# The four residual norms of a three-layer network kernel: the last tile's sums read from its PSUM bank, the sums of seven tiles placed within the last weight chunk, and the VectorE chain rewritten without operations on two SBUF operands

## The chip, the core and the metric

The kernel runs on one core of one Trainium2 chip. The metric is the device time of one execution in microseconds (us), as the median of repeated runs; lower is better.

## The reference, cut to what matters

The program is a network of three layers on 512 tokens with a model width of 1024, all in fp32. The first two layers end each of their halves in a normed, gated residual; the second half of the chain is the norm ahead of the next projection:

```
def rms_normalize(x):
    xf = x.astype(jnp.float32)
    return xf * lax.rsqrt(jnp.mean(xf * xf, axis=-1, keepdims=True) + EPS)

for i in range(DEPTH):                       # DEPTH = 2
    h = rmsnorm(x, norm_g[i, 0]) * (1.0 + scale) + shift
    y = short_conv_mixer(...) if i == 0 else ssd_mixer(...)
    x = x + gate * rmsnorm(y, norm_g[i, 1])
    h = rmsnorm(x, norm_g[i, 2]) * (1.0 + scale2) + shift2
    y = swiglu_ffn(h, f_w_in[i], f_w_out[i])
    x = x + gate2 * rmsnorm(y, norm_g[i, 3])
```

So there are four places, here called norm 0 to norm 3, at which a projection y (8 tiles of 128 channels by 512 tokens) becomes the new x, and the new x is normalised for the next projection. A third layer (attention and a gated FFN) follows, with norms of another form that the change does not touch.

## The kernel before, in words

Activations lie with the channels on the 128 partitions and the tokens along the free axis; a tile is 128x512. A projection multiplies fp32 weights in three products (high part by high part, high by low, low by high), so one tile with 8 k tiles takes 24 matmuls of 128x512. Weights stream through a ring of 4 chunks: SP loads `raw`, ScalarE writes the rounded part `whi` (`split_hi`), GpSimd writes the rest `wlo` (`split_lo`, 128x1024), and TensorE's `chunk` waits for it. Each engine has its own instruction list in program order, written by hand, and the lists meet only at semaphores.

A projection's tile m goes to bank `(T0 + m) % 4`. At the end of the four projections with a residual norm (`a_out`, `f_out0`, `m_out`, `f_out1`), ScalarE (`y_out`) squares tile m from the bank, writes y = gate column times the bank, and squares y; VectorE (`residual_sums`) forms x*y and adds three running sums over the tiles: `sums[0]` of the raw squares, `sums[1]` of x*y, `sums[2]` of y squared. For tile 7 the squares are added into `sums[0]`, while x*y stays in `ta` and the square of y in `tb`.

Then comes the chain of the norm. TensorE (`residual_roots`) sums over the channels with `token_sums`: the data is the stationary operand and a column of ones moves, 4 matmuls per buffer, each of which the trace shows as two records. There are five such buffers: `sums[1]`, `sums[2]`, `sums[0]`, `ta`, `tb`. ScalarE takes the square root of the first sum; VectorE inverts it (`R1`), squares the inverse (`R1SQ`), and combines the sums into the mean square of the new x (`PART`, `LAST`, `ssum`), without waiting for the new x itself; ScalarE takes that root, and VectorE inverts it (`R2`). TensorE spreads `R1` and `R2` over the partitions (`spread`, 4 matmuls of 128x128 each, in two records apiece) into banks 6 and 4. VectorE then forms, for each k, `grown` (y times bank 6, into `sq`), `added` (x plus that) and `scaled` (x times bank 4), ScalarE writes `h_hi` and `tb` from it, and GpSimd `h_lo`. TensorE takes them in the order of k in `four`, whose first matmul (line 566) waits for the first `h_hi`; it also waits for the low parts of the next projection's first four chunks.

In ScalarE's list `y_tile` sets, for the last tile, `y_out`, then one `split_hi`, and after it the roots:

```
done(c + chunks - 1)
y_out(name, r, m, y, sums)
split_hi(c + RING + chunks - 1)
```

Of the kernel before, what the change touches and what calls it, by code (L numbers as in the profile page):

```python
# [25 lines left out]
P = 128  # L26
# [97 lines left out]
def program(nc, io):  # L124
    with ExitStack() as ctx:
# [26 lines left out]
        root = sb("root", [P, 7, NT])  # L152
# [92 lines left out]
        s_done, s_ready, std_out, r_ready, rb_done = (sem(n) for n in ("s_done", "s_ready", "std_out", "r_ready", "rb_done"))  # L245
# [85 lines left out]
        STD, R1, R1SQ, PART, LAST, R2, SPARE = range(7)  # L331
# [199 lines left out]
        def _(pe):  # L531
            PRODUCTS = ((whi, "hi"), (whi, "lo"), (wlo, "hi"))

            def chunk(c, it, n, bank, ktiles, k0, xs, first, last, wait_in=None):

                s = c % RING
                pe.wait_ge(lo_ready, c + 1 + it * n)
                for kk in range(ktiles):
                    k = k0 + kk
                    if wait_in is not None:  # L540
                        pe.wait_ge(in_ready, wait_in + k + 1)
                    for i, (w, part) in enumerate(PRODUCTS):
                        mm = nc.tensor.matmul(psum[bank][:], w[:, s, kk, :], xs[part == "lo"][:, k, :],  # L543
                                              start=first and kk == 0 and i == 0,
                                              stop=last and kk == ktiles - 1 and i == 2)
                mm.then_inc(chunk_done, 1)
# [8 lines left out]
            def single(name, u, it=0, n=0, xs=(h_hi, h_lo), wait=True, c=None):  # L555

                b = bank_of(T0[name] + u, it, n)
                chunk(C0[name] + (u if c is None else c), it, n, b, CH, 0, xs, True, True, I0[name] if wait else None)
# [36 lines left out]
            def down(name, it, xs):  # L595

                for m in range(4):
                    b = bank_of(T0[name] + m, it, 4)
                    k = 0
                    for u, n in enumerate((6, 5, 6, 5)):  # L600
                        chunk(C0[name] + 4 * m + u, it, 16, b, n, k, xs, u == 0, u == 3, I0[name] if m == 0 else None)
# [17 lines left out]
            def residual_roots(r, sums):  # L619

                pe.wait_ge(acc_c, 6 * (r + 1))
                token_sums(5, sums[:, 1, :], True)
                token_sums(4, sums[:, 2, :], True)
                pe.wait_ge(acc_a, 7 * (r + 1))
                token_sums(6, sums[:, 0, :], True).then_inc(s_done, 1)
                pe.wait_ge(xy_out, r + 1)
                token_sums(5, ta[:, 1, :], False).then_inc(s_done, 1)
                pe.wait_ge(yc_out, KD * (r + 1))
                token_sums(4, tb[:, 1, :], False).then_inc(s_done, 1)
# [58 lines left out]
            for u in range(KD):  # L688
                single("a_out", u, xs=(g_hi, g_lo))
                if u == 0:  # L690
                    modulation(10)
            residual_roots(0, sums)

            def ffn(n):
# [21 lines left out]
                with pe.Fori(0, 2) as it:  # L716
                    down(f"f_out{n}", it, (g_hi, g_lo))
                residual_roots(1 + 2 * n, sums)
# [117 lines left out]
            for m in range(4, KD):  # L836
                b = bank_of(T0["m_out"] + m)
                for u in range(2):
                    chunk(C0["m_out"] + 2 * m + u, 0, 0, b, CH, CH * u, (m_hi, m_lo), u == 0, u == 1)
            residual_roots(2, sums_m)  # L840
# [194 lines left out]
        def _(act):  # L1035
# [25 lines left out]
            def residual_roots(r):  # L1061

                act.wait_ge(s_done, sums_done(r, 0))
                take_root(roots(r, 0), psum[6][:, 0:NT])
# [33 lines left out]
            def y_out(name, r, m, y, sums):  # L1098
# [5 lines left out]
                if m >= 3:  # L1104
                    act.wait_ge(acc_a, 7 * r + m - 2)
                dst = sq[:, m % 2, :] if m else sums[:, 0, :]
                nc.scalar.activation(dst, psum[b][:], ACT.Square).then_inc(ya_out, 1)  # L1107
                nc.scalar.activation(y[:, m, :], psum[b][:], ACT.Identity, bias=zcol[:], scale=ncol[:, r, 1, m:m + 1]).then_inc(bank_free[b], 1)
# [372 lines left out]
        def _(dve):  # L1481
# [21 lines left out]
            def residual_sums(name, r, y, sums):  # L1503

                for m in range(KD):
                    t = T0[name] + m
                    if m:
                        dve.wait_ge(ya_out, KD * r + m + 1)
                        if m >= 2:
                            dve.wait_ge(acc_a, 7 * r + m - 1)  # L1510
                        TT(sums[:, 0, :], sums[:, 0, :], sq[:, m % 2, :], ALU.add).then_inc(acc_a, 1)  # L1511
                    read_out(t)
                    if m == KD - 1:
                        TT(ta[:, 1, :], x[:, m, :], y[:, m, :], ALU.mult).then_inc(xy_out, 1)
                        return
                    step(TT(ta[:, m % 2, :] if m else sums[:, 1, :], x[:, m, :], y[:, m, :], ALU.mult))
                    if m:
# [4 lines left out]
                        TT(sums[:, 2, :], sums[:, 2, :], tb[:, m % 2, :], ALU.add).then_inc(acc_c, 1)  # L1522

# [12 lines left out]
            def residual(r, i, phase, y):  # L1536

                inverse(roots(r, 0), R1)
                step(TT(root[:, R1SQ, :], root[:, R1, :], root[:, R1, :], ALU.mult))
                dve.wait_ge(s_done, sums_done(r, 1))  # L1540
                step(STT(out=root[:, PART, :], in0=psum[5][:, 0:NT], scalar=2.0, in1=root[:, R1, :], op0=ALU.mult, op1=ALU.mult))
                step(TT(root[:, PART, :], root[:, PART, :], ssum[:], ALU.add))
                dve.wait_ge(s_done, sums_done(r, 2))
                step(TT(root[:, LAST, :], psum[4][:, 0:NT], root[:, R1SQ, :], ALU.mult))
                TT(ssum[:], root[:, LAST, :], root[:, PART, :], ALU.add).then_inc(s_ready, 1)
                inverse(roots(r, 1), R2)

                def grown(k):
                    return step.note(TT(sq[:, k % 2, :], y[:, k, :], psum[6][:], ALU.mult))

                def added(k, v):
                    step.wait(v)
                    return step.note(TT(x[:, k, :], x[:, k, :], sq[:, k % 2, :], ALU.add))  # L1553
# [148 lines left out]
            residual(0, 1, "f_in0", y)  # L1702

            def ffn(n):
# [33 lines left out]
                residual(1 + 2 * n, 2 + 2 * n, ("m_in", "w_in")[n], y)  # L1738
# [166 lines left out]
            residual(2, 3, "f_in1", y_m)  # L1905
# [300 lines left out]
```

## Time and profile before

| | |
|---|---|
| time, median of 3 runs | 2298.25 us (2295.49 to 2298.49) |
| time of the profiled execution | 2297.04 us |
| its span, first to last instruction | 2295.2 us |
| mean granted TensorE clock | 0.978 |
| TensorE matmul busy | 2223.1 us (97%), 10434 instructions |
| VectorE busy | 1242.6 us (54%) |
| ScalarE busy | 994.1 us (43%) |
| GpSimd busy | 974.2 us (42%) |

The profiled execution lasted 1.84 us longer than its span. TensorE is nearly always busy. The stretches of the four norms lie at 226 to 238 us, 622 to 635 us, 1100 to 1112 us and 1484 to 1496 us of the span. The granted clock is given as a share of full speed: 1.00 is 2.4 GHz, 0.50 is 1.2 GHz. The program's other time is the same loop of weight chunks and the third layer's attention.

### The profile page before, as it was taken

The numbers are of one execution on the slowest core, as the hardware profiler recorded it, in microseconds if no ns is written. First come the engines' busy times: TensorE is split into PE (matmuls) and PEld (weight loads), VectorE is DVE, ScalarE is ACT, GpSimd is POOL, SyncE is SP. The second block draws the span as 40 slices with busy tenths as digits, with TensorE's granted clock in tenths as the row PEclk, the third lists the DMA queues.
The fourth block names the chain that finished last, engine by engine and source line by source line (L and its number), as shares of the span: only waits on it lengthen the run. The fifth ranks groups of instructions, "written<-read, shape, count | busy, mean of one in ns | idle before, by whom it ended". The sixth has DMA issues, their size and how long they took to land.

```text
span 2295.2 us, 28959 instructions
## 1 busy us (share of the span) xinstructions
PE 2223.1 (97%) x10434; PEld 1761.0 (77%) x10434; DVE 1242.6 (54%) x1718; ACT 994.1 (43%) x1420; POOL 974.2 (42%) x421
## 2 busy tenths in 40 slices
PE   6999999999979999989999999999999899999998
PEld 4788888788867777767788888878677688888886
DVE  5876666521297787786522221250777755666412
ACT  4324443333435546554534334453555634444332
POOL 3544443446534333334444446556211143444563
PEclk8999899999989999999899999999999999999999
DMA  7553475553315344332133223334321032333232
GB/s 304 212 202 125 152 265 201 185 143 95 115 40 186 111 142 149 113 111 90 59 103 97 91 72 95 109 106 145 97 67 47 29 107 76 108 93 91 76 91 72
DMA packets 74096, 273.83 MB, mean 119 GB/s; under 512 B 8519, under 2 KB 11207, under 8 KB 67736
## 3 DMA queue, kind: packets, MB, share of 16 engines
q1 hardware_dynamic: 70632, 266.74, 35.6%
q10 hardware_dynamic: 3376, 5.90, 0.8%
q8 instruction: 57, 0.93, 0.2%
q14 instruction: 31, 0.25, 0.0%
HBM read 269.21 MB, written 8.12 MB: 121 GB/s over the span
## 4 chain that ended last, share of the span: by engine, by line
PE 76%; issue 14%; POOL 5%; DVE 3%; ACT 1%; DMA 0%; ACTq 0%; POOLq 0%; SPq 0%; DVEq 0%
PE bank L543 60%; POOL wlo L504 5%; PE bank L913 4%; PE bank L566 2%; PE bank L1006 2%; PE bank L970 1%; PE bank L934 1%; PE bank L953 1%; PE bank L570 1%; PE bank L607 1%; PE bank L615 1%; PE bank L654 1%; PE bank L854 0%; DVE x L1553 0%; DMA ada_first<-ada_d 0%
## 5 line engine op out<-in xcount | busy, mean ns | idle before, releaser
L504 POOL TENSOR_TENSOR wlo<-raw,whi 128x1024 fp32r<-128x1024 f32 x382 | 928.8, 2438 | 1235.9 <-ACT whi L1044 1235.7
L1044 ACT ACTIVATE whi<-raw 128x1024 fp32r<-128x1024 f32 x382 | 401.3, 1055 | 622.9 <-PE bank L543 588.3
L543 PE MATMUL bank<-h_hi,whi 128*128 128x512 f32 x1616 | 649.3, 402 | 4.9 <-DVE dt_tok L1878 2.5
L543 PE MATMUL bank<-h_hi,wlo 128*128 128x512 f32 x1616 | 638.1, 395 | 0.0
L543 PE MATMUL bank<-h_lo,whi 128*128 128x512 f32 x1616 | 636.0, 394 | 0.0
L543 PEld LDWEIGHTS bank<-h_hi,whi 128*128 128x128 f32 x1616 | 303.9, 188 | 79.6 <-issue 5.7
L543 PEld LDWEIGHTS bank<-h_hi,wlo 128*128 128x128 f32 x1616 | 303.8, 188 | 77.2
L543 PEld LDWEIGHTS bank<-h_lo,whi 128*128 128x128 f32 x1616 | 304.0, 188 | 70.4
L543 PE MATMUL bank<-g_hi,whi 128*128 128x512 f32 x592 | 236.3, 399 | 0.0
L543 PE MATMUL bank<-g_hi,wlo 128*128 128x512 f32 x592 | 233.2, 394 | 0.0
L543 PE MATMUL bank<-g_lo,whi 128*128 128x512 f32 x592 | 232.1, 392 | 0.0
L1713 DVE TENSOR_TENSOR tb<-ta,bank 128x512 f32<-128x512 f32 x44 | 30.1, 685 | 222.3 <-PE bank L543 202.7
L1495 DVE TENSOR_TENSOR g_lo<-tb,g_hi 128x512 f32 (+1 forms) x52 | 109.1, 2098 | 51.9 <-ACT g_hi L1173 45.0
L543 PEld LDWEIGHTS bank<-g_hi,wlo 128*128 128x128 f32 x592 | 111.1, 188 | 29.1
L543 PEld LDWEIGHTS bank<-g_lo,whi 128*128 128x128 f32 x592 | 111.1, 188 | 26.4
L543 PEld LDWEIGHTS bank<-g_hi,whi 128*128 128x128 f32 x592 | 111.1, 188 | 25.4
L1511 DVE TENSOR_TENSOR sums<-sums,sq 128x512 f32<-128x512 f32 x21 | 14.5, 692 | 193.2 <-ACT sq L1107 193.1
L1652 DVE SCALAR_TENSOR_TENSOR tb<-bank,vec,tb 128x511 f32<-128x511 f32 (+1 forms) x140 | 104.8, 749 | 9.8
L566 PE MATMUL bank<-h_hi,whi 128*128 128x512 f32 x160 | 68.2, 426 | 9.2 <-ACT h_hi L1089 7.0
L1843 DVE TENSOR_TENSOR csb<-csb,cbm 128x1280 f32<-128x1280 f32 x32 | 72.0, 2288 | 0.3
L519 POOL TENSOR_TENSOR h_lo<-tb,h_hi 128x512 fp32r<-128x512 f32 x35 | 45.2, 1293 | 59.9 <-ACT tb L1090 59.6
L566 PE MATMUL bank<-h_hi,wlo 128*128 128x512 f32 x160 | 67.2, 420 | 0.0
(337 smaller groups left out, 2953.5 us busy)
## 6 DMA issues: line engine op xcount, KB each, us to landing
raw<-f_in_d SPq DMA_DIRECT2D x88, 512.0 KB, 3.5
raw<-m_d SPq DMA_DIRECT2D x65, 512.0 KB, 3.7
ada_f<-ada_d SPq DMA_DIRECT2D x24, 1024.0 KB, 7.0
raw<-g_in_d SPq DMA_DIRECT2D x44, 512.0 KB, 3.5
raw<-w_in_d SPq DMA_DIRECT2D x41, 512.0 KB, 3.6
csb<-cs_d SPq DMA_DIRECT2D x32, 640.0 KB, 6.5
ada_a<-ada_d SPq DMA_DIRECT2D x16, 1024.0 KB, 4.9
raw<-a_in_d SPq DMA_DIRECT2D x24, 512.0 KB, 6.0
```

The source lines that it names most:

```text
L504: nc.gpsimd.tensor_tensor(wlo[:, s], raw[:, s], whi[:, s].bitcast(F32), ALU.subtract).then_inc(lo_ready, 1)
L519: nc.gpsimd.tensor_tensor(h_lo[:, k, :], tb[:, k % 2, :], h_hi[:, k, :].bitcast(F32), ALU.subtract).then_inc(in_ready, 1)
L543: mm = nc.tensor.matmul(psum[bank][:], w[:, s, kk, :], xs[part == "lo"][:, k, :], start=first and kk == 0 and i == 0, stop=last and kk == ...
L566: nc.tensor.matmul(psum[tiles[i]][:], w[:, (C0[name] + i) % RING, k, :], h_hi[:, k, :], start=k == 0 and j == 0, stop=False)
L570: mm = nc.tensor.matmul(psum[tiles[i]][:], whi[:, (C0[name] + i) % RING, k, :], h_lo[:, k, :], start=False, stop=k == KD - 1)
L913: mm = nc.tensor.matmul(psum[7][:], w[:, c % RING, m // 3, :], (h_hi, h_lo)[part == "lo"][:, m // 3, :], start=m == 0, stop=m == 23)
L1006: mm = nc.tensor.matmul(psum[b][:], w[:, c % RING, k, :], (h_hi, h_lo)[part == "lo"][:, k, :], start=kk == 0 and i == 0, stop=kk == 3 and ...
L1044: nc.scalar.activation(whi[:, s], raw[:, s], ACT.Copy).then_inc(hi_ready, 1)
L1495: TT(dst, whole, hi.bitcast(F32), ALU.subtract).then_inc(in_ready, 1)
L1652: ins = STT(out=out[:, d:S], in0=src[:, 0:S - d], scalar=col(width - 1 - d), in1=out[:, d:S], op0=ALU.mult, op1=ALU.add)
L1713: TT(tb[:, j % 2, :], ta[:, j % 2, :], psum[b][:], ALU.mult).then_inc(bank_free[b], 1)
L1843: TT(csb[:, r, :], csb[:, r, :], cbm[:], ALU.mult).then_inc(m_done, 1)
```

## The change

Three edits, made at all four norms.

1. The token sums of `sums[0]`, `sums[1]` and `sums[2]`, which now cover tiles 0 to 6, are issued by TensorE ahead of the last k tile of the projection's last chunk (`late`, `sums_so_far`), so three matmuls of 128x512 follow them.
2. Tile 7 is handled from its bank: ScalarE squares it into `sq`, squares it again with the gate column as scale into `tb`, and VectorE multiplies bank, gate column and x into `ta` in one operation, which waits for ScalarE's second square. ScalarE writes y of tile 7 only when that operation has finished, since both read one bank. The token sums of `sq`, `tb` and `ta` (in this order) are added to banks 6, 4 and 5.
3. On the chain, ScalarE writes the root and then its square (`VAR`), and VectorE inverts both with one reciprocal (`R1` and `R1SQ`). `ssum` is copied to PSUM bank 7, and sums pass through banks; `grown` writes to banks 5 and 7 rather than to `sq`, and `added` reads them there. No VectorE operation from the last tile's product to `added` reads two SBUF operands any more.

For the order of the lists, `f_out`'s loop of 2 turns on TensorE is written out. Cut to its core (arguments passed through and the counts of `acc_a`, now 6 a norm, are left out in part):

```
@@ -328,7 +329,7 @@
 
 
 
-        STD, R1, R1SQ, PART, LAST, R2, SPARE = range(7)
+        STD, VAR, R1, R1SQ, PART, LAST, R2, SPARE = range(8)
 
...
@@ -531,12 +532,14 @@
         def _(pe):
             PRODUCTS = ((whi, "hi"), (whi, "lo"), (wlo, "hi"))
 
-            def chunk(c, it, n, bank, ktiles, k0, xs, first, last, wait_in=None):
+            def chunk(c, it, n, bank, ktiles, k0, xs, first, last, wait_in=None, late=None):
 
                 s = c % RING
                 pe.wait_ge(lo_ready, c + 1 + it * n)
                 for kk in range(ktiles):
                     k = k0 + kk
+                    if late is not None and kk == ktiles - 1:
+                        sums_so_far(*late)
                     if wait_in is not None:
                         pe.wait_ge(in_ready, wait_in + k + 1)
                     for i, (w, part) in enumerate(PRODUCTS):
@@ -552,10 +555,10 @@
                     pe.wait_ge(bank_free[b], t // 4 + it * (n // 4))
                 return b
...
-            def down(name, it, xs):
-
-                for m in range(4):
+            def down(name, it, xs, first=0, late=None):
+
+                for m in range(first, first + 4):
                     b = bank_of(T0[name] + m, it, 4)
                     k = 0
                     for u, n in enumerate((6, 5, 6, 5)):
-                        chunk(C0[name] + 4 * m + u, it, 16, b, n, k, xs, u == 0, u == 3, I0[name] if m == 0 else None)
+                        chunk(C0[name] + 4 * m + u, it, 16, b, n, k, xs, u == 0, u == 3, I0[name] if m == 0 else None,
+                              late if m == KD - 1 and u == 3 else None)
                         k += n
...
-            def residual_roots(r, sums):
-
+            def sums_so_far(r, sums):
+
+                pe.wait_ge(acc_a, 6 * (r + 1))
                 pe.wait_ge(acc_c, 6 * (r + 1))
-                token_sums(5, sums[:, 1, :], True)
-                token_sums(4, sums[:, 2, :], True)
-                pe.wait_ge(acc_a, 7 * (r + 1))
-                token_sums(6, sums[:, 0, :], True).then_inc(s_done, 1)
+                for bank, j in ((6, 0), (5, 1), (4, 2)):
+                    token_sums(bank, sums[:, j, :], True)
+
+            def residual_roots(r):
+
+                pe.wait_ge(ya_out, KD * (r + 1))
+                token_sums(6, sq[:, 1, :], False).then_inc(s_done, 1)
+                pe.wait_ge(yc_out, KD * (r + 1))
+                token_sums(4, tb[:, 1, :], False).then_inc(s_done, 1)
                 pe.wait_ge(xy_out, r + 1)
                 token_sums(5, ta[:, 1, :], False).then_inc(s_done, 1)
-                pe.wait_ge(yc_out, KD * (r + 1))
-                token_sums(4, tb[:, 1, :], False).then_inc(s_done, 1)
                 spread(6, roots(r, 0), R1)
                 spread(4, roots(r, 1), R2)
...
-                with pe.Fori(0, 2) as it:
-                    down(f"f_out{n}", it, (g_hi, g_lo))
-                residual_roots(1 + 2 * n, sums)
+                down(f"f_out{n}", 0, (g_hi, g_lo))
+                down(f"f_out{n}", 0, (g_hi, g_lo), 4, (1 + 2 * n, sums))
+                residual_roots(1 + 2 * n)
...
@@ -1061,7 +1070,9 @@
             def residual_roots(r):
 
                 act.wait_ge(s_done, sums_done(r, 0))
-                take_root(roots(r, 0), psum[6][:, 0:NT])
+                nc.scalar.activation(root[:, STD, :], psum[6][:, 0:NT], ACT.Sqrt, bias=epscol[:], scale=1.0 / D).then_inc(root_out, 1)
+                act.wait_ge(root_out, r + 1)
+                nc.scalar.activation(root[:, VAR, :], root[:, STD, :], ACT.Square).then_inc(std_out, 1)
                 act.wait_ge(s_ready, r + 2)
                 take_root(roots(r, 1), ssum[:])
 
@@ -1102,9 +1113,17 @@
                 if m == 0:
                     act.wait_ge(gate_ready, r + 1)
                 if m >= 3:
-                    act.wait_ge(acc_a, 7 * r + m - 2)
+                    act.wait_ge(acc_a, 6 * r + m - 2)
                 dst = sq[:, m % 2, :] if m else sums[:, 0, :]
                 nc.scalar.activation(dst, psum[b][:], ACT.Square).then_inc(ya_out, 1)
+                if m == KD - 1:
+
+                    act.wait_ge(acc_c, 6 * r + m - 2)
+                    nc.scalar.activation(tb[:, m % 2, :], psum[b][:], ACT.Square, scale=ncol[:, r, 1, m:m + 1]).then_inc(yc_out, 1)
+                    act.wait_ge(xy_out, r + 1)
+                    nc.scalar.activation(y[:, m, :], psum[b][:], ACT.Identity, bias=zcol[:],
+                                         scale=ncol[:, r, 1, m:m + 1]).then_inc(bank_free[b], 1)
+                    return
                 nc.scalar.activation(y[:, m, :], psum[b][:], ACT.Identity, bias=zcol[:], scale=ncol[:, r, 1, m:m + 1]).then_inc(bank_free[b], 1)
                 read_out(t)
...
@@ -1502,17 +1521,14 @@
 
             def residual_sums(name, r, y, sums):
 
-                for m in range(KD):
+                for m in range(KD - 1):
                     t = T0[name] + m
                     if m:
                         dve.wait_ge(ya_out, KD * r + m + 1)
                         if m >= 2:
-                            dve.wait_ge(acc_a, 7 * r + m - 1)
+                            dve.wait_ge(acc_a, 6 * r + m - 1)
                         TT(sums[:, 0, :], sums[:, 0, :], sq[:, m % 2, :], ALU.add).then_inc(acc_a, 1)
                     read_out(t)
-                    if m == KD - 1:
-                        TT(ta[:, 1, :], x[:, m, :], y[:, m, :], ALU.mult).then_inc(xy_out, 1)
-                        return
                     step(TT(ta[:, m % 2, :] if m else sums[:, 1, :], x[:, m, :], y[:, m, :], ALU.mult))
                     if m:
                         step(TT(sums[:, 1, :], sums[:, 1, :], ta[:, m % 2, :], ALU.add))
@@ -1520,6 +1536,11 @@
                         if m >= 2:
                             dve.wait_ge(acc_c, 6 * r + m - 1)
                         TT(sums[:, 2, :], sums[:, 2, :], tb[:, m % 2, :], ALU.add).then_inc(acc_c, 1)
+                step(nc.vector.tensor_copy(psum[7][:, 0:NT], ssum[:]))
+                m = KD - 1
+                dve.wait_ge(yc_out, KD * (r + 1))
+                STT(out=ta[:, m % 2, :], in0=psum[(T0[name] + m) % 4][:], scalar=ncol[:, r, 1, m:m + 1], in1=x[:, m, :],
+                    op0=ALU.mult, op1=ALU.mult).then_inc(xy_out, 1)
...
-            def residual(r, i, phase, y):
-
-                inverse(roots(r, 0), R1)
-                step(TT(root[:, R1SQ, :], root[:, R1, :], root[:, R1, :], ALU.mult))
+            def residual(r, name, i, phase, y):
+
+                dve.wait_ge(std_out, roots(r, 0) + 1)
+                nc.vector.reciprocal(root[:, R1:R1SQ + 1, :], root[:, STD:VAR + 1, :]).then_inc(r_ready, 1)
+                dve.wait_ge(r_ready, roots(r, 0) + 1)
                 dve.wait_ge(s_done, sums_done(r, 1))
+                step(TT(root[:, LAST, :], psum[4][:, 0:NT], root[:, R1SQ, :], ALU.mult))
+                dve.wait_ge(s_done, sums_done(r, 2))
                 step(STT(out=root[:, PART, :], in0=psum[5][:, 0:NT], scalar=2.0, in1=root[:, R1, :], op0=ALU.mult, op1=ALU.mult))
-                step(TT(root[:, PART, :], root[:, PART, :], ssum[:], ALU.add))
-                dve.wait_ge(s_done, sums_done(r, 2))
-                step(TT(root[:, LAST, :], psum[4][:, 0:NT], root[:, R1SQ, :], ALU.mult))
-                TT(ssum[:], root[:, LAST, :], root[:, PART, :], ALU.add).then_inc(s_ready, 1)
+                step(TT(psum[7][:, NT:2 * NT], psum[7][:, 0:NT], root[:, PART, :], ALU.add))
+                TT(ssum[:], psum[7][:, NT:2 * NT], root[:, LAST, :], ALU.add).then_inc(s_ready, 1)
                 inverse(roots(r, 1), R2)
+                read_out(T0[name] + KD - 1)
 
                 def grown(k):
-                    return step.note(TT(sq[:, k % 2, :], y[:, k, :], psum[6][:], ALU.mult))
+                    return step.note(TT(psum[(5, 7)[k % 2]][:], y[:, k, :], psum[6][:], ALU.mult))
 
                 def added(k, v):
                     step.wait(v)
-                    return step.note(TT(x[:, k, :], x[:, k, :], sq[:, k % 2, :], ALU.add))
+                    return step.note(TT(x[:, k, :], x[:, k, :], psum[(5, 7)[k % 2]][:], ALU.add))
 
```

## Rows read from the trace of the kernel before

**Rows 1.** The page's chain that ended last, by line:

```profile
PE bank L543 60%; POOL wlo L504 5%; PE bank L913 4%; PE bank L566 2%; PE bank L1006 2%; PE bank L970 1%; PE bank L934 1%; PE bank L953 1%; PE bank L570 1%; PE bank L607 1%; PE bank L615 1%; PE bank L654 1%; PE bank L854 0%; DVE x L1553 0%; DMA ada_first<-ada_d 0%
```

**Rows 2.** Timeline of TensorE at norm 0: start us, duration us, instructions merged:

```profile
226.65 0.39 PE L543 MATMUL bank<-g_hi,wlo 128*128 128x512 f32 x1
226.88 2.73 PE L607 MATMUL bank<-ones,sums 128*128 128x1 f32 x24
229.48 1.29 PE L607 MATMUL bank<-ones,ta 128*128 128x1 f32 x8
230.63 1.85 PE L607 MATMUL bank<-ones,tb 128*128 128x1 f32 x8
232.34 3.76 PE L615 MATMUL bank<-kst,root 128*128 128x128 f32 x16
237.88 0.77 PE L566 MATMUL bank<-h_hi,whi 128*128 128x512 f32 x1 [1.78 <-ACT h_hi L1089]
...
246.21 0.39 PE L566 MATMUL bank<-h_hi,whi 128*128 128x512 f32 x1
```

**Rows 3.** Timeline of ScalarE at norm 0:

```profile
227.08 0.60 ACT L1107 ACTIVATE sq<-bank 128x512 f32<-128x512 f32 x1 [2.71 <-PE bank L543]
227.57 0.77 ACT L1108 ACTIVATE y<-bank,zcol,ncol 128x512 f32<-128x512 f32 x1
...
228.91 1.04 ACT L1044 ACTIVATE whi<-raw 128x1024 fp32r<-128x1024 f32 x1
229.86 0.24 ACT L1055 ACTIVATE root<-bank,epscol 128x4 f32<-128x4 f32 x1
```

**Rows 4.** Timeline of GpSimd at norm 0:

```profile
230.03 2.35 POOL L504 TENSOR_TENSOR wlo<-raw,whi 128x1024 fp32r<-128x1024 f32 x1 [2.84 <-ACT whi L1044]
```

**Rows 5.** Timeline of VectorE at norm 0:

```profile
230.35 2.04 DVE L1539 TENSOR_TENSOR root<-root 128x4 f32<-128x4 f32 x1
...
233.02 0.16 DVE L1545 TENSOR_TENSOR ssum<-root 128x4 f32<-128x4 f32 x1
```

**Rows 6.** Timeline of TensorE at norms 1, 2 and 3:

```profile
622.89 0.39 PE L543 MATMUL bank<-g_hi,wlo 128*128 128x512 f32 x1
...
634.38 0.47 PE L566 MATMUL bank<-h_hi,whi 128*128 128x512 f32 x1 [1.78 <-ACT h_hi L1089]
...
640.20 0.39 PE L566 MATMUL bank<-h_hi,whi 128*128 128x512 f32 x1
...
1100.42 0.39 PE L543 MATMUL bank<-m_hi,wlo 128*128 128x512 f32 x1
...
1111.53 0.77 PE L566 MATMUL bank<-h_hi,whi 128*128 128x512 f32 x1 [1.72 <-ACT h_hi L1089]
...
1484.57 0.39 PE L543 MATMUL bank<-g_hi,wlo 128*128 128x512 f32 x1
...
1491.69 2.08 PE L615 MATMUL bank<-kst,root 128*128 128x128 f32 x8 [0.85 <-DVE root L1500]
1495.49 0.77 PE L566 MATMUL bank<-h_hi,whi 128*128 128x512 f32 x1 [1.72 <-ACT h_hi L1089]
```

**Rows 7.** Busy time by stretch after norm 0; the clock stands behind the five engines:

```profile
238.00:241.00 3.00, 3.00 (x7) 2.33 (x8) 3.00 (x6) 1.96 (x3) 1.31 (x2) 0.50 0.73 306
247.00:250.00 3.00, 3.00 (x15) 2.41 (x14) 3.00 (x5) 2.05 (x4) 1.29 (x1) 1.00 0.00 0
```

**Rows 8.** Timeline of TensorE about one `modulation` within a chunk stream:

```profile
79.64 0.95 PE L654 MATMUL bank<-ones,modacc 128*128 128x1 f32 x8
80.45 0.48 PE L543 MATMUL bank<-h_hi,whi 128*128 128x512 f32 x1
```

**Rows 9.** Groups by line: count, then duration in ns (min/median/max):

```profile
L2067 DVE SCALAR_TENSOR_TENSOR y<-x,vec,bank x8: 739/739/746, 2287.2 to 2291.9; 128x512 f32<-128x512 f32 x8
L1553 DVE TENSOR_TENSOR x<-x,sq x32: 691/1086/1429, 235.2 to 1508.4; 128x512 f32<-128x512 f32 x32
L1055 ACT ACTIVATE root<-ssum,epscol x5: 297/298/298, 23.3 to 1491.1; 128x4 f32<-128x4 f32 x5
```

More of the change, by code:

```diff
@@ L151, in program @@
         tb = sb("tb", [P, 2, S])
-        root = sb("root", [P, 7, NT])
+        root = sb("root", [P, 8, NT])
         ssum = sb("ssum", [P, NT])
@@ L244, in program @@
             sem(n) for n in ("gate_ready", "ya_out", "yc_out", "acc_a", "acc_c", "xy_out", "x2_out", "acc_x"))
-        s_done, s_ready, std_out, r_ready, rb_done = (sem(n) for n in ("s_done", "s_ready", "std_out", "r_ready", "rb_done"))
+        s_done, s_ready, root_out, std_out, r_ready, rb_done = (
+            sem(n) for n in ("s_done", "s_ready", "root_out", "std_out", "r_ready", "rb_done"))
         dve_step = sem("dve_step")
@@ L553, in bank_of, with single @@
                 return b
-            def single(name, u, it=0, n=0, xs=(h_hi, h_lo), wait=True, c=None):
+            def single(name, u, it=0, n=0, xs=(h_hi, h_lo), wait=True, c=None, late=None):
                 b = bank_of(T0[name] + u, it, n)
-                chunk(C0[name] + (u if c is None else c), it, n, b, CH, 0, xs, True, True, I0[name] if wait else None)
+                chunk(C0[name] + (u if c is None else c), it, n, b, CH, 0, xs, True, True, I0[name] if wait else None, late)
             def four(name, n):
@@ L688, in _ @@
             for u in range(KD):
-                single("a_out", u, xs=(g_hi, g_lo))
+                single("a_out", u, xs=(g_hi, g_lo), late=(0, sums) if u == KD - 1 else None)
                 if u == 0:
                     modulation(10)
-            residual_roots(0, sums)
+            residual_roots(0)
             def ffn(n):
@@ L838, in _ @@
                 for u in range(2):
-                    chunk(C0["m_out"] + 2 * m + u, 0, 0, b, CH, CH * u, (m_hi, m_lo), u == 0, u == 1)
-            residual_roots(2, sums_m)
+                    chunk(C0["m_out"] + 2 * m + u, 0, 0, b, CH, CH * u, (m_hi, m_lo), u == 0, u == 1,
+                          late=(2, sums_m) if (m, u) == (KD - 1, 1) else None)
+            residual_roots(2)
             ffn(1)
@@ L1701, in _ @@
             residual_sums("a_out", 0, y, sums)
-            residual(0, 1, "f_in0", y)
+            residual(0, "a_out", 1, "f_in0", y)
             def ffn(n):
@@ L1737, in ffn @@
                 residual_sums(f_out, 1 + 2 * n, y, sums)
-                residual(1 + 2 * n, 2 + 2 * n, ("m_in", "w_in")[n], y)
+                residual(1 + 2 * n, f_out, 2 + 2 * n, ("m_in", "w_in")[n], y)
             dve.wait_ge(brow_wr, 16)
@@ L1904, in _ @@
             residual_sums("m_out", 2, y_m, sums_m)
-            residual(2, 3, "f_in1", y_m)
+            residual(2, "m_out", 3, "f_in1", y_m)
             ffn(1)
```

## Prediction

> **What bounds the kernel now.** I read four views. First the page's chain that ended last: it is TensorE's chunk stream (line 543 holds 60%), and the norm's own lines, the token sums (607) and the spreads (615), have 1% each [rows 1]. So the chunk stream runs at TensorE's pace, and whatever is put into it is paid in full. The four norms are the places where TensorE can't go on, so the question is what ends last there.
>
> Second, the timeline of TensorE at the norms. I measure from L, the start of the projection's last matmul, to H, the start of the first matmul that reads the new `h_hi`. At norm 0 this is 226.65 to 237.88, 11.23 us [rows 2]; at norm 1 11.49, at norm 2 11.11, at norm 3 10.92 [rows 6]. The sum is 44.75 us, the mean 11.19: all that the chain's three edits can work on.
>
> What fills it: 40 records of token sums from 226.88 to 232.34, and then 16 records of spreads, with no idle time between [rows 2]. TensorE itself is the last to finish at norm 0, and in the same pattern at norms 1 and 2 (three of four). Only norm 3 differs: TensorE sits idle for 0.85 us ahead of the second spread, waiting for `R2` [rows 6].
>
> Why is TensorE so slow there? The first 24 records start 2.60 us before the next group (0.108 us each), while the 8 of `tb` take 1.71 us from start to next start, 0.214 each, and a spread's record 0.235 [rows 2]. The clock has fallen to its lower level, 1.2 GHz, within some 4 us after the last wide matmul, although TensorE was at work on one-column matmuls all along, and it is still there when the new projection starts: 0.50 in 238 to 241 us, with 7 matmuls in 3 us, against 15 at 1.00 (2.4 GHz) later [rows 7].
>
> Third, VectorE: the square of the inverse, 4 columns wide, takes 2.04 us [rows 5]; the other operations of this size take 0.16. It ends at 232.39, GpSimd's `split_lo` at 232.38 [rows 4]: two SBUF operands wait out GpSimd's instruction. But the first spread doesn't need this result, and the second had its `R2` in time at three norms. The stall is real and stands beside TensorE's work; taken away alone, it is worth about 0.85 us at norm 3 and nothing elsewhere. The Trainium skill (SBUF — State Buffer, Who interferes with whom) says the same: a VectorE instruction with two SBUF inputs contends with a GpSimd instruction that reads SBUF, one with a single SBUF input does not. By it the new chain has no such stall, as I reckon below too.
>
> **The change, part by part.**
>
> *Sums into the stream.* 24 records leave the gap and stand ahead of the last three matmuls. In the gap they took 2.60 us [rows 2]. Within a stream, 8 records of `modulation` span 0.81 us (0.10 each), and the matmul behind them lasts 0.48 instead of 0.39 [rows 8]. Bounds: 24 x 0.10 = 2.4 and 2.60 + 0.1 = 2.7; I take 2.70, as these are the same records. No gain hides in a wait here, since the stream has none. `acc_c` of tile 6 is ready before (tile 7's matmuls take 5.6 us at norm 0, 24 x 0.233, and more at the others). So the new start of the last matmul is L' = L + 2.70.
>
> *The gap after L': ScalarE and VectorE.* ScalarE's square starts 0.43 after L' (226.65 to 227.08), the next activation 0.49 later [rows 2, 3]. The second square from the bank was not in the trace: nearest are 0.60 (square from a bank) and 0.77 (bank with a column as scale) [rows 3]; I take 0.77, ending at L' + 1.69. VectorE's product of bank, column and x: 0.74 by the same operation elsewhere [rows 9], ending at 2.47. Only then may y be written, 0.70 later `split_hi` starts (3.2), and the root starts 0.95 behind that, since `split_hi` stands ahead of it in the list [rows 3]: L' + 4.14, against L + 3.21 before. The root takes 0.24; its square in 4 columns lies between nothing less than 0.2 and the 0.30 of the row for 4 SBUF columns [rows 9], I take 0.25; with a hop of 0.04 each way and the reciprocal (0.18) `R1` is there at about L' + 4.9 and the first spread may start at L' + 4.95. Queued behind y's wait are thus `split_hi` and the root, and with `split_hi` GpSimd's `split_lo`, for which the next projection's first matmul waits too: it would end near L' + 6.7, well ahead of H, so this costs nothing.
>
> *The gap after L': TensorE.* There are now three buffers to sum, not two (the raw square of tile 7 is no longer added by VectorE): 24 records, so 48 in all where 40 were. They can't start before ScalarE's first square, L' + 1.08, so TensorE sits idle for 0.85 us first. At the upper clock they take 2.6 us and end well before `R1`. At the lower they take 3 x 1.71 = 5.13 [rows 2] and end at L' + 6.21, later than `R1`.
>
> *From the spreads to H:* 232.34 to 237.88, 5.54 us [rows 2], at the lower clock. VectorE's four small operations now end 0.8 us after the reciprocal (232.39 to 233.18 before [rows 5]), so `R2` follows within some 1.4 us of `R1`, before the first spread (about 1.9 us) is over: the wait of norm 3 goes, and VectorE's chain is nowhere last.
>
> *Sum.* Two cases a norm. Case A, ScalarE's order sets the pace: 2.70 + 4.95 + 5.54 = 13.19 us from L to H. Case B, TensorE's sums at the lower clock do: 2.70 + 6.21 + 5.54 = 14.45. Against 44.75, four of A give +8.0 us and four of B +13.1. The clock fell at norms 0 to 2 between 3 and 4 us behind L, which is about L' + 1 now, as the one-column records begin as early as before; at norm 3 it fell later (its first wait on `R2` and the second spread, 2.08 us for 8 records [rows 6]). So I take three B and one A: 43.35 + 13.19 - 44.75 = +11.8 us.
>
> The Trainium skill (TensorE: Matmul & The Clock Gate, What's actually happening) has TensorE's clock halved after an idle stretch and restored by sustained work. It speaks against this change, which adds idle time ahead of the last sums; by it all norms would be B, +13.1.
>
> *In `four`.* `added` has a median of 1.09 us and 0.69 without contention [rows 9]; it saves VectorE up to 0.4 x 32 = 13 us in all. I cost this at nothing: a turn of k there is 12 matmuls, two turns took 5.82 us at norm 1 from the first (634.38 to 640.20) [rows 6], which is 24 matmuls at 0.233 with 0.2 to spare, so TensorE covers it. If that cover were gone it would be worth up to those 13 us. `grown` and `added` through banks cost as before, by the 0.74 and 0.69 us of operations with a bank. The slow matmuls of `four` (two turns took 8.33 us at norm 0 [rows 2], 5.82 at norm 1, so 2.5 us for the clock) I leave as they are; bounds are one such norm more (+2.5) and one less (-2.5).
>
> *The loop written out:* no gap was seen at the loop's turn, so nothing either way.
>
> The profiled execution took 2297.04 us, so the sum is 2308.8. The median of the runs stands 1.2 us above it; I stay with the sum.
>
> **The rivals.**
> 1. *The clock stays at 2.4 GHz through the gap,* because the wide matmuls now stand nearer to the spreads. Then the first spread starts at L' + 4.95, `R2` is there at 6.3, the second spread takes half of 2.08, and H comes at 6.3 + 1.04 + 1.78 = L' + 9.1: 11.8 from L, +2.5 us in all; and three norms lose their 2.5 us of slow matmuls in `four`, -7.5. Together -5.0: 2292.0. It decides the sign as soon as the clock holds to the end of `four`'s first turns at three norms. Against it: the clock fell at every norm, with TensorE less idle than it would be now. Chance 0.04.
> 2. *VectorE paces `four`.* It was busy 3.00 of 3.00 us there [rows 7]. Then up to 13 us come back: about 2296 to 2298. Against it the even turns of TensorE. 0.04.
> 3. *The sums in the stream cost next to nothing* (they fill gaps of weight loading). Then +11.8 - 10.8 = +1.0: 2298. Rows 8 speak against it. 0.03.
> 4. *The clock falls within the sums*, before the last three matmuls: up to 2.6 us more a norm, 2319. The sums alone last 2.6 us, and the clock held longer than that at all norms. 0.04.
>
> **How the numbers follow.** The forecast, between all A and all B, has 0.83; 0.02 is left for what I don't see, half of it on each side of no change. The range takes all A less 2.5 us and something for the runs' spread of 3 us, and all B with 2.5 us more: 2301.5 to 2314. About 0.2% (4.6 us) is what a measurement of this kernel can tell from no change. Faster by more: rival 1 and half of the rest, 0.05. Within: rivals 2 and 3 and a tail of the forecast, 0.08. Slower: 0.87.
>
> **What would show it.** In the profile after: 24 records on `sums` ahead of the last three matmuls and some 2.6 us long; ScalarE's order square, square, y, `split_hi`, root, with the root 4.1 us behind the last matmul's start; no small VectorE operation above 0.3 us; 24 records of `sq`, `tb`, `ta` at about 0.21 us each at most norms and the first spread right behind them; H 14.4 us behind L (13.2 where the clock is up). The prediction is wrong if the spreads' records take half as long, if H comes at under 12 us from L, or if a stretch far from the norms changes.

## The result: 12 us slower, and the profile after

The changed kernel takes 2310.72 us (median of 4 runs, 2309.93 to 2312.3) against 2298.37 us for the kernel before, measured beside it: a ratio of 1.0058, 95% interval 1.0045 to 1.0071. The forecast was 2308.8, range 2301.5 to 2314.0.

The profiled span grew from 2295.2 to 2308.7 us, by 13.5. Where that lies is read at the four norms, in the timeline of TensorE. At norm 1 of the changed kernel (the first line is the tail of the 24 records in the stream):

```profile
627.26 0.25 PE L611 MATMUL bank<-ones,sums 128*128 128x1 f32 x1
627.37 0.48 PE L546 MATMUL bank<-g_hi,whi 128*128 128x512 f32 x1
627.69 0.39 PE L546 MATMUL bank<-g_lo,whi 128*128 128x512 f32 x1
627.92 0.40 PE L546 MATMUL bank<-g_hi,wlo 128*128 128x512 f32 x1
629.00 1.87 PE L611 MATMUL bank<-ones,sq 128*128 128x1 f32 x8 [0.69 <-ACT sq L1118]
630.73 1.84 PE L611 MATMUL bank<-ones,tb 128*128 128x1 f32 x8
632.44 1.84 PE L611 MATMUL bank<-ones,ta 128*128 128x1 f32 x8
634.14 3.76 PE L619 MATMUL bank<-kst,root 128*128 128x128 f32 x16
640.00 0.76 PE L569 MATMUL bank<-h_hi,whi 128*128 128x512 f32 x1 [2.09 <-ACT h_hi L1100]
```

From the last matmul (627.92) to the first new one (640.00) it is 12.08 us, where norm 1 of before has 11.49 [rows 6], although 24 records of sums have left the gap. They stand in the stream, and TensorE sums three buffers behind it, each at 1.71 us from start to start: the lower clock holds from the first of them. The spreads follow without a gap.

ScalarE at the same norm:

```profile
628.35 0.60 ACT L1118 ACTIVATE sq<-bank 128x512 f32<-128x512 f32 x1 [5.05 <-PE bank L546]
628.85 0.68 ACT L1122 ACTIVATE tb<-bank,ncol 128x512 f32<-128x512 f32 x1
630.42 0.78 ACT L1124 ACTIVATE y<-bank,zcol,ncol 128x512 f32<-128x512 f32 x1 [0.90 <-DVE ta L1542]
631.10 1.04 ACT L1053 ACTIVATE whi<-raw 128x1024 fp32r<-128x1024 f32 x1
632.05 0.25 ACT L1073 ACTIVATE root<-bank,epscol 128x4 f32<-128x4 f32 x1
```

The root starts 4.13 us behind the last matmul; in the kernel before it was 3.21 [rows 2, 3]. y waits for VectorE's product, and the weight split and the root stand behind y. But this is not what ends last, as VectorE shows:

```profile
632.57 0.20 DVE L1560 RECIPROCAL root<-root 128x8 f32<-128x8 f32 x1 [2.18 <-ACT root L1075]
632.81 0.16 DVE L1563 TENSOR_TENSOR root<-bank,root 128x4 f32<-128x4 f32 x1
634.39 0.16 DVE L1565 SCALAR_TENSOR_TENSOR root<-bank,root 128x4 f32<-128x4 f32 x1 [1.42 <-PE bank L611]
...
635.32 0.18 DVE L1519 RECIPROCAL root<-root 128x4 f32<-128x4 f32 x1 [0.36 <-ACT root L1064]
```

`R1` is there at 632.77, the first spread starts at 634.14: for 1.4 us the inverse waits for TensorE, which is still summing. VectorE too waits 1.42 us, for the sum of `ta`. The 2.04 us stall [rows 5] is gone, and so is all contention in `four`: `added`, whose median was 1086 ns [rows 9], is now

```profile
L1576 DVE TENSOR_TENSOR x<-x,bank x32: 680/681/687, 238.8 to 1519.9; 128x512 f32<-128x512 f32 x32
```

and VectorE's busy time fell from 1242.6 to 1219.6 us. No gain from it can be measured (experiment 3).

The four norms, in us, from the timelines of TensorE. L is the start of the projection's last matmul; for the changed kernel the inserted time stands by itself (the last matmul's start less that of the fourth last, less the 0.70 that three matmuls take):

| | norm 0 | norm 1 | norm 2 | norm 3 | sum |
|---|---|---|---|---|---|
| before: L to the first new matmul | 11.23 | 11.49 | 11.11 | 10.92 | 44.75 |
| after: inserted into the stream | 2.78 | 2.68 | 2.68 | 2.68 | 10.82 |
| after: last matmul to the first new one | 11.95 | 12.08 | 11.36 | 11.68 | 47.07 |
| before: two turns of `four` | 8.33 | 5.82 | 8.42 | 7.66 | 30.23 |
| after: two turns of `four` | 7.22 | 8.20 | 7.40 | 7.10 | 29.92 |

10.82 + 47.07 - 44.75 = +13.14 us, the turns -0.31, and 0.7 us of the 13.5 lie elsewhere: 0.6 between norms 1 and 2. The stretches of both `f_out` projections, whose loop was written out, are as long as before (376.68 us from the turns of norm 0 to the last matmul of norm 1's projection, less the insertion, and 364.62 from norm 2 to norm 3, in both traces).

### The profile page after: what moved, and what is told of

It is laid out like the page before. It is cut to its first block, busy times and chain, and to the rows that moved or that the text cites. A ratio compares the mean times of both kernels' runs of the same rounds, so it can differ in the third digit from the quotient of the medians.

```text
span 2308.7 us, 28949 instructions
## 1 busy us (share of the span) xinstructions
PE 2234.8 (97%) x10466; PEld 1771.4 (77%) x10466; DVE 1219.6 (53%) x1714; ACT 994.6 (43%) x1424; POOL 974.7 (42%) x421
## 4 chain that ended last, share of the span: by engine, by line
PE 76%; issue 15%; POOL 5%; DVE 3%; ACT 1%; DMA 0%; ACTq 0%; POOLq 0%; SPq 0%; DVEq 0%
PE bank L546 59%; POOL wlo L505 5%; PE bank L922 4%; PE bank L569 2%; PE bank L1015 2%; PE bank L611 1%; PE bank L979 1%; PE bank L943 1%; PE bank L573 1%; PE bank L962 1%; PE bank L662 1%; PE bank L619 1%; PE bank L863 0%; PE bank L652 0%; DMA x<-x_d 0%
```

## The experiments

All were run in five rounds beside the kernel before. Where matmuls are added, their results are unused; no experiment leaves out a part of the computation. "Kernel 3" below is that of experiment 3.

**1. The sums back into the gap.** The changed kernel, the token sums of tiles 0 to 6 behind the last matmul:

```
                 for kk in range(ktiles):
                     k = k0 + kk
-                    if late is not None and kk == ktiles - 1:
-                        sums_so_far(*late)
...
-            def residual_roots(r):
+            def residual_roots(r, sums=sums):
 
+                sums_so_far(r, sums)
                 pe.wait_ge(ya_out, KD * (r + 1))
```

> The changed kernel, with the token sums of tiles 0 to 6 issued behind the last matmul instead of within the last chunk; all else as changed. Theory (what stands in the stream is paid in full, and behind it TensorE's sums at 1.2 GHz set the pace): the 24 records overlap with ScalarE's squares, so 2.7 us leave the stream and the sums end 1.1 to 1.7 us later behind the last matmul; about 1 us less a norm, 4 to 6 us less than changed, 2304 to 2307. Rival (ScalarE's order, square, square, y, split, root, sets the pace): the full 2.7 us a norm come back, 2300.

Measured: 2304.14 us, ratio 1.0030 (1.0019 to 1.0041). TensorE at norm 1 of this kernel:

```profile
624.93 0.39 PE L544 MATMUL bank<-g_hi,wlo 128*128 128x512 f32 x1
625.16 2.90 PE L609 MATMUL bank<-ones,sums 128*128 128x1 f32 x24
627.92 1.85 PE L609 MATMUL bank<-ones,sq 128*128 128x1 f32 x8
629.63 1.84 PE L609 MATMUL bank<-ones,tb 128*128 128x1 f32 x8
631.33 1.85 PE L609 MATMUL bank<-ones,ta 128*128 128x1 f32 x8
633.04 3.76 PE L617 MATMUL bank<-kst,root 128*128 128x128 f32 x16
638.89 0.77 PE L567 MATMUL bank<-h_hi,whi 128*128 128x512 f32 x1 [2.09 <-ACT h_hi L1099]
```

TensorE is never idle up to the end of the spreads, and at no norm is ScalarE last. The four gaps sum to 51.60 us (12.84, 13.96, 12.26, 12.54), against 57.89 with the insertion: placing the sums in the stream costs 6.3 us by the gaps and 6.4 by the ratios (1.0058 - 1.0030), a little more than the 4 to 6 I expected. Two turns of `four` took 2.7 us less in this trace too (27.18 against 29.92), but 4.3 us more lie far from the norms, where the clock also fell at times in this execution. So one trace's span doesn't give a difference of a few us; the gaps do for their own stretch. The rival, by which ScalarE's order sets the pace, fell: 2300 did not come.

**2. The root first on ScalarE.** The changed kernel:

```
                     nc.scalar.activation(tb[:, m % 2, :], psum[b][:], ACT.Square, scale=...).then_inc(yc_out, 1)
+                    act.wait_ge(s_done, sums_done(r, 0))
+                    nc.scalar.activation(root[:, STD, :], psum[6][:, 0:NT], ACT.Sqrt, ...).then_inc(root_out, 1)
+                    act.wait_ge(root_out, r + 1)
+                    nc.scalar.activation(root[:, VAR, :], root[:, STD, :], ACT.Square).then_inc(std_out, 1)
                     act.wait_ge(xy_out, r + 1)
```

> The changed kernel, with ScalarE's root and its square ahead of y and of the weight split of the last tile. Theory (TensorE's 24 records of sums at the lower clock are last, and the root has 1.4 us of slack behind them): no change to the changed kernel within 1 us, 2310. Rival (ScalarE's order is last): the root comes some 1.4 us earlier a norm, 5 us less, 2305.

Measured: 2311.72 us, ratio 1.0053 (1.0039 to 1.0067). The intervals of this and of the changed kernel overlap. But the five runs fall apart: three took 2311.72 to 2312.35 us, at a mean granted clock of 0.975, and two took 2306, near the rival's number, at 0.980 and 0.979. The trace is of the run of 2312.35, and no trace shows the other two, so the times alone don't settle it. The trace does, for its execution: the root came earlier behind the last matmul (at norm 0 at 232.36, 2.71 us behind it), and the gaps are 11.49, 12.08, 11.35, 11.67. At norms 1 to 3 they are within 0.02 us of the changed kernel's; at norm 0 the gap is 0.46 shorter, and there the clock fell 1.4 us behind the last matmul's start, where in the changed kernel it fell 0.3 us ahead of it. ScalarE's order is not what ends last.

**3. The chain's edit alone.** The kernel before, with ScalarE's square of the root, one reciprocal, and the sums and `grown` through banks, as in the change; tile 7 and the token sums untouched.

```
+                dve.wait_ge(std_out, roots(r, 0) + 1)
+                nc.vector.reciprocal(root[:, R1:R1SQ + 1, :], root[:, STD:VAR + 1, :]).then_inc(r_ready, 1)
-                inverse(roots(r, 0), R1)
-                step(TT(root[:, R1SQ, :], root[:, R1, :], root[:, R1, :], ALU.mult))
```

> The kernel before, with the chain's edit alone (one reciprocal for both inverses, ScalarE's square of the root, ssum and grown through banks; tile 7 and all token sums as before). Theory (VectorE's 2.04 us stall stands beside TensorE's work at three of four norms): the small operation falls to 0.2 us, the time by 0 to 1.5 us, 2297 to 2298. Rival (the stall is on the path): 2 us a norm, 8 us less, 2290.

Measured: 2295.2 us against 2296.41, ratio 0.9997 (0.9988 to 1.0007). No difference that can be measured. TensorE at norm 3, the only one where it had been idle for `R2` [rows 6]:

```profile
1486.60 1.03 PE L608 MATMUL bank<-ones,ta 128*128 128x1 f32 x8
1487.49 1.79 PE L608 MATMUL bank<-ones,tb 128*128 128x1 f32 x8
1489.14 3.76 PE L616 MATMUL bank<-kst,root 128*128 128x128 f32 x16
1494.62 0.77 PE L567 MATMUL bank<-h_hi,whi 128*128 128x512 f32 x1 [1.72 <-ACT h_hi L1092]
```

The idle 0.85 us is gone, but the clock fell earlier there, and the gap is 10.85 where it was 10.92. The four gaps sum to 43.64, against 44.75.

**4. Two of the three early sums alone.** The kernel before:

```
+            def sums_so_far(r, sums):
+
+                pe.wait_ge(acc_c, 6 * (r + 1))
+                token_sums(5, sums[:, 1, :], True)
+                token_sums(4, sums[:, 2, :], True)
```

called ahead of the last k tile of the last chunk, and taken from `residual_roots` (`f_out`'s loop is written out, as in the change).

> The kernel before, with the token sums of sums[1] and sums[2] (16 records) within the last chunk and everything else as before. Theory: 1.8 us a norm are added to the stream; behind it TensorE waits for VectorE's last addition into sums[0] and sums 24 records at the lower clock, 12.5 us to the first new matmul against 11.2: 3.1 us a norm, 2310. Rival (early sums shorten the gap by what they take): no change, 2298.

Measured: 2308.65 us, ratio 1.0055 (1.0041 to 1.0068). The insertion is 1.78 us at each norm, and the gaps are 12.02, 12.18, 12.43 and 11.12: with less work in the gap it got longer at each norm, since TensorE now sits idle for 1.41 us until VectorE has added tile 7's square, and starts its 24 records later. At norms 0 to 2 the clock fell before or within the first 8 of them; at norm 3 it fell within the second 8, and there the gap grew least, by 0.20 us.

**5. One more token sum.** Kernel 3, with 8 records more in the gap, into a free bank:

```
                 token_sums(5, ta[:, 1, :], False).then_inc(s_done, 1)
+                token_sums(bank_of(T0[("f_in0", "m_in", "f_in1", "w_in")[r]]), sums[:, 2, :], True)
```

> The kernel before with the chain's edit and one more token sum (8 records, result unused, into a free bank) between those of ta and tb. Theory (TensorE's records are last, at 0.21 us each at the lower clock): 1.7 us more a norm, less where the clock falls later, 5.5 to 6.8 us more than with the chain's edit alone: 2301 to 2302. Rival (the chain of ScalarE and VectorE is last once the records are few): 2296 to 2297.

Measured: 2303.17 us against 2297.76, ratio 1.0026 (1.0015 to 1.0038); by the ratios 6.7 us more than kernel 3. At norm 0:

```profile
229.09 1.34 PE L608 MATMUL bank<-ones,ta 128*128 128x1 f32 x8
230.29 1.84 PE L608 MATMUL bank<-ones,sums 128*128 128x1 f32 x8
232.00 1.84 PE L608 MATMUL bank<-ones,tb 128*128 128x1 f32 x8
```

The added group takes its full 1.71 us. The four gaps sum to 51.06 us, 7.4 more than kernel 3's 43.64, and within 0.6 of experiment 1's 51.60, though single norms differ by up to 1.6 us either way. By the ratios experiment 1 is 0.9 us slower than this kernel, which is within the error. So a third buffer alone (in experiment 1 the last tile's raw square, no longer added by VectorE) accounts for what experiment 1 has over kernel 3, as far as these runs can tell.

**6. Wide matmuls between the sums, to hold the clock.** A helper was added to the changed kernel, to kernel 3 and to the kernel before:

```
+            def fill(r, n):
+                name = ("f_in0", "m_in", "f_in1", "w_in")[r]
+                slot = C0[name] % RING
+                if n < 0:
+                    pe.wait_ge(lo_ready, C0[name] + 1)
+                    bank_of(T0[name])
+                    n = -n
+                for i in range(n):
+                    nc.tensor.matmul(psum[T0[name] % 4][:], whi[:, slot, 4, :],
+                                     whi[:, slot, 0:4, :].rearrange("p k m -> p (k m)"), start=True, stop=True)
```

> The changed kernel with wide matmuls (128x512, result unused, into a free bank) put between TensorE's sums and spreads at each norm: 3 behind the last matmul, 2 behind each of the three sums and the first spread, 6 behind the second spread. Theory (the lower clock makes the gap long and the first turns slow): where they hold the clock at 2.4 GHz, the sums take 0.9 us each, the first new matmul comes 9.2 us behind the last one instead of 11.8, and the slow matmuls behind it lose 6.6 us in all: 2294. Rival (the clock is not held by this, or is not what costs): the added matmuls take 0.43 us each on the path, 2315 to 2326.

> The kernel before with the chain's edit and wide matmuls between the sums (1 behind each of the five sums and the first spread, 6 behind the second spread). Theory (clock): 9.8 us from the last matmul to the first new one against 11.2, and 6.9 us of slow matmuls gone: about 2284. Rival (clock not held): 2 to 2.5 us more a norm, 2305.

> The same wide matmuls in the kernel before, without the chain's edit. Theory: once TensorE is no longer last, VectorE's 2.04 us stall is: the first new matmul comes no earlier than 9.9 us behind the last one, 0.2 to 0.5 us a norm later than with the chain's edit: about 2285 to 2286. Rival (the clock is not held): as without the chain's edit, 2305.

Measured: 2312.49 us (ratio 1.0056, 1.0042 to 1.0070) for the changed kernel, 2296.71 (0.9997, 0.9988 to 1.0006) for kernel 3, and 2299.91 (1.0006, 0.9997 to 1.0015) for the kernel before. My numbers and the rivals' were missed in all three: the clock was held through all the sums at only two of the twelve norms, norm 2 of the changed kernel and norm 1 of kernel 3. Gaps of the changed kernel with it: 14.24, 14.63, 10.97, 15.19. The one short gap shows what holding would be worth, and where it ended; norm 2:

```profile
1114.86 1.05 PE L611 MATMUL bank<-ones,sq 128*128 128x1 f32 x8
1115.77 0.70 PE L639 MATMUL bank<-whi 128*128 128x512 f32 x2
1116.31 0.95 PE L611 MATMUL bank<-ones,tb 128*128 128x1 f32 x8
...
1119.37 1.91 PE L619 MATMUL bank<-kst,root 128*128 128x128 f32 x8
```

Here 8 records last 0.95 us as at full clock, and the clock falls only at the end of the last sum (the spread's 8 records take 1.91 us). At the other norms of this kernel two added matmuls take about 1.0 us on the path. But one half of the theory came true everywhere: two turns of `four` took 5.68 to 5.85 us at all 12 norms of the three kernels, which is full clock from the start. That led to the next three.

**7. Wide matmuls behind the second spread only.** There TensorE sits idle for 1.8 us before the first new `h_hi`, so 4 of them cost nothing even at the lower clock:

```
                 spread(4, roots(r, 1), R2)
+                fill(r, -4)
```

> The kernel before with the chain's edit, and 4 wide matmuls (result unused, free bank) behind the second spread only, where TensorE otherwise sits idle for 1.8 us. Theory: the spreads and these keep TensorE busy up to the new projection, so the clock returns earlier and two turns take 5.8 us at most norms instead of 5.8 to 7.4 (27.5 us for the four norms with the chain's edit alone): up to 4 us less than with the chain's edit alone, 2291 to 2293, faster than both kernels. Rival (the clock's return isn't moved by them): 2295 to 2296.

> The same 4 wide matmuls in the kernel before. Theory: 30.2 us for two turns at the four norms fall towards 23.3: 3 to 6 us less, 2291 to 2293. Rival: no change, 2297.

> The same 4 wide matmuls in the changed kernel. Theory: 29.9 us for two turns at the four norms fall towards 23.3, the gap stays: 3 to 6 us less than changed, 2305 to 2308. Rival: no change, 2310 to 2311.

Measured: with kernel 3's edit 2289.85 us, ratio 0.9967 (0.9955 to 0.9979); in the kernel before 2292.7, 0.9982 (0.9973 to 0.9991); in the changed kernel 2305.18, 1.0038 (1.0025 to 1.0052). In the traces two turns of `four` fell from 27.51, 30.23 and 29.92 us in all (without these matmuls) to 23.44, 23.46 and 23.46, while the gaps' sums went from 43.64 to 43.96, from 44.75 to 46.70, and from 47.07 to 47.02: -3.8, -4.8 and -6.5 us. By the ratios the gains are 6.9, 4.1 and 4.6 us, uncertain by 3.5, 2 and 4 us; the first is more than I had forecast. Norm 0 of the first:

```profile
233.35 3.48 PE L616 MATMUL bank<-kst,root 128*128 128x128 f32 x16
236.59 1.17 PE L629 MATMUL bank<-whi 128*128 128x512 f32 x4
238.77 0.47 PE L567 MATMUL bank<-h_hi,whi 128*128 128x512 f32 x1 [1.01 <-ACT h_hi L1105]
239.08 0.39 PE L567 MATMUL bank<-h_hi,wlo 128*128 128x512 f32 x1
```

The new projection's matmuls start 0.31 and then 0.23 us apart, where in the kernel before they took twice that [rows 2, 7]. Two turns of `four` take 5.8 to 6.0 us at all four norms in each of the three kernels. The first two are faster than the kernel before and the changed kernel. Where the clock stood when the added matmuls began differs: at four of the twelve norms it was back just before them (at norm 0 above the granted clock is 0.50 up to 236.4 us and 1.00 from there, with the first of them at 236.59), at five it rose while they ran, and at three within the new projection's second matmul. At none did it fall again in these turns, as it did in the changed kernel at norm 0, where it was up from 239.4 us and fell at 242.8, 1.4 us into the new projection.

Norm 2 of the first kernel shows the rest: the clock happened to hold nearly to the end of `tb`'s sum there, and the gap is 10.05 us.

```profile
1101.68 1.03 PE L608 MATMUL bank<-ones,ta 128*128 128x1 f32 x8
1102.57 1.11 PE L608 MATMUL bank<-ones,tb 128*128 128x1 f32 x8
1103.54 3.58 PE L616 MATMUL bank<-kst,root 128*128 128x128 f32 x16
```

## Why the prediction was right, point by point

*TensorE is last in the gap, and the stream's records are paid in full.* Right, and shown by experiments 1, 4 and 5. The insertion was sized at 2.70 us and measured 2.68 at three norms and 2.78 at norm 0, where the clock fell within the last two matmuls (0.54 and 0.63 us long). That is a small instance of rival 4.

*ScalarE's order.* Its times were right (root 4.13 against 4.14; the second square 0.68 where I took 0.77, the square of the root 0.21 where I took 0.25), and it is not last: experiment 2.

*TensorE's three sums at the lower clock.* Right in kind. I had 11.75 us for such a gap and measured a mean of 11.77 (47.07 / 4). That the mean fits so well is in part luck: norm 1 is 0.33 longer, with 2.09 us of waiting for the first `h_hi` where I had 1.78 (why stays open), and norm 2 is 0.39 shorter, since the clock fell within its first sum. The step that was mis-sized is "three B and one A": norm 3 was case B as well (11.68, not 10.49), and so the sum was 1.26 us short. Had I taken all four as B, I would have said +13.1, with 13.14 measured. My ground for A was that the clock fell later at norm 3, 5.0 us behind the last matmul. But the one-column records begin right behind that matmul in the kernel before, and 3.15 us (norm 0: 3.26) ahead of it in the changed kernel. Counted from the first of them, the clock fell after 3.2, 2.9, 3.3 and 4.8 us at norms 0 to 3 of the kernel before and after 3.0, 3.7, 4.6 and 4.3 us in the changed one. Even 4.8 us is only 1.7 us behind the changed kernel's last matmul, with most of the three sums still to come. So the trace of the kernel before already spoke for B at norm 3.

The Trainium skill (TensorE: Matmul & The Clock Gate, What's actually happening), which has the clock halved after idle time, spoke for B at all four norms, and B came, but this trace doesn't show idle time as its cause everywhere: at norm 0 of the changed kernel the clock fell at 229.1 us, with TensorE at work up to 230.0, and in the kernel before it fell at all four norms with no idle time behind the last matmul. Where the two differ, the measurement decides: idle time was not needed.

*`R2`.* I put it some 1.4 us behind `R1`; at norm 1 it came 2.73 us behind (632.77 to 635.50), since `PART` waits for TensorE's sum of `ta`. It was still ahead of the second spread, so this didn't show.

*VectorE's stall.* Right: gone in the profile, not on the path. Experiment 3 moves the time by less than can be measured. With wide matmuls in place, the kernels with the chain's edit are 2.9 us (2289.85 against 2292.7) and 3.2 us (2296.71 against 2299.91) ahead of those without it. These differences are uncertain by some 3 us, and TensorE was never idle for `R2` in the four traces, so the stall was not last there either. Where the clock happened to fall differs between them (the gaps of one kernel differ by 1.8 us from norm to norm), and these runs don't give the edit's own worth.

*The rule on two SBUF operands.* The Trainium skill (SBUF — State Buffer, Who interferes with whom) holds here on both sides: `added` went from 1086 ns to 681, and no small VectorE operation of the chain takes more than 0.204 us where one took 2.04, with GpSimd's `split_lo` running beside them as before (at norm 1 from 632.22 us, for 2.34).

*`four`.* Costed at nothing, measured at -0.31 us for the slow turns. VectorE's 23 us less were hidden, as forecast: at full clock two turns take 5.83 us with the old `added` and with the new one (experiment 7, second and first kernel), so rival 2 fell. Rival 1's -7.5 us was slightly too much: by the table the slow turns of the kernel before cost 7.0 us in all over full clock (30.23 less 4 x 5.82). Rivals 1 and 3 fell with the lower clock at all four norms, the insertion's 2.68 us and experiment 4.

The parts of the change, by the ratios to the kernel before (times 2298 us): the chain's edit -0.7 (not measurable), tile 7 from its bank +7.6 (1.0030 - 0.9997), mostly its third token sum; the early place of the sums +6.4 (1.0058 - 1.0030). These sum to +13.3, where the medians differ by 12.35; each part is uncertain by 2 to 4 us. The gaps of the traces give -1.1, +8.0 and +6.3, or +13.1.

What stays open: why the clock fell 2.9 us behind the first one-column record at one norm and 4.8 us behind it at another. No run here controls it.

## What to carry to other kernels

Work moved out of a wait and into a stream that already runs at the pace of its engine is not hidden; it is paid in full, while the wait may stay as long as before if another chain, or the same engine's remaining work, ends it. A stall of 2 us on an engine is worth removing only if the next thing in line isn't already busy for longer: compare the ends, not the lengths. And where TensorE is idle ahead of a new projection, a few wide matmuls with an unused result in that idle time made the projection start at full clock, for 4 to 7 us less in all over four places.

## What the runs showed that I had not expected

TensorE's clock fell to 1.2 GHz while TensorE was busy without a pause. These are two stretches of norm 0 of the kernel before, in columns as in rows 7 (TensorE's busy time stands first, and the granted clock behind the five engines):

```profile
228.50:230.00 1.50, 1.50 (x15) 1.50 (x15) 0.57 (x1) 1.50 (x3) 0.00 (x0) 1.00 0.75 279
230.20:233.20 3.00, 3.00 (x15) 3.00 (x16) 2.81 (x6) 0.00 (x0) 2.18 (x1) 0.50 0.00 0
```

TensorE is busy for all of both, and the clock goes from 1.00 to 0.50 between them. One-column matmuls, 24 records in 2.6 us, didn't keep it up, nor did one wide matmul behind every 8 of them (experiment 6, where it fell at all norms of kernel 3, at norm 1 only in the first spread). A one-column fp32 record took 0.108 us at 2.4 GHz and 0.214 at 1.2 GHz, so sums over channels on TensorE, written as one-column matmuls, cost twice as much just where they are waited for. With wide matmuls behind the spreads it was back by the new projection's second matmul at all 12 norms of experiment 7, whichever kernel they stood in. Of the 28 norms in the seven traces without any added wide matmuls, seven had two turns of `four` at full clock (5.8 us).
